# A hybrid diffusion layer on one core: new order of the FFN's head and turn, 19 of its 20 full pairs by Strassen's scheme, activations reloaded on GpSimd's queue

## The reference, cut to what matters

```
def _convffn(h, rows, l, p):
    up = jnp.einsum('bld,df->blf', h, p['ffn_w_up'][l])      # 1024 -> 2 x 2816
    up = _dwconv3(up, p['ffn_conv_w'][l], rows)              # width-3 conv along tokens
    gate, val = jnp.split(up, 2, axis=-1)
    return jnp.einsum('blf,fd->bld', jax.nn.silu(gate) * val, p['ffn_w_down'][l])
...
    x = x + g2 * _convffn(h, rows, l, p)
...
    y_sample = _rmsnorm(xs, final_norm_w)
```

## Time and profile before

| what | value |
|---|---|
| median of 3 runs | 944.24 us (943.34 to 944.41) |
| the profiled execution: time | 944.79 us |
| its span, first to last instruction | 943.0 us |
| PE busy | 901.4 us (96%) |
| DVE busy | 699.2 us (74%) |
| ACT busy | 438.0 us (46%) |
| mean granted TensorE clock | 0.986 |

### The profile page before, as it was taken

One profiled execution on the slowest core, in us unless ns is written; L12 is line 12 of the kernel. 1 busy time (PEld: TensorE's weight loads), 2 busy tenths in 40 slices (PEclk: granted clock), 3 DMA queues, 4 the chain that ended last, 5 costly groups with the idle time before them and its releaser, 6 DMA issues. The chain is left out here.

```text
span 943.0 us, 14067 instructions
## 1 busy us (share of the span) xinstructions
PE 901.4 (96%) x5410; PEld 797.9 (85%) x5410; DVE 699.2 (74%) x884; ACT 438.0 (46%) x713; POOL 39.1 (4%) x58
## 2 busy tenths in 40 slices
PE   7999999999999999999996999999999999987997
PEld 3479898898998988687795999999999999975885
DVE  5744666957858856898678798789779878976536
ACT  5754433333433333232656555555555555553353
POOL 2100000100000000001000000000000000000000
PEclk9999999999999999999997999999999999998999
DMA  9664323423422353218021213322331332215813
GB/s 321 210 219 150 127 75 135 132 79 126 146 95 90 135 179 89 107 24 223 0 90 53 101 59 126 117 87 91 104 118 64 136 110 98 73 65 190 278 48 113
DMA packets 39275, 112.76 MB, mean 120 GB/s; under 512 B 4471, under 2 KB 12663, under 8 KB 38568
## 3 DMA queue, kind: packets, MB, share of 16 engines
q1 hardware_dynamic: 33944, 93.58, 29.1%
q0 software_dynamic: 4800, 17.99, 6.2%
q10 hardware_dynamic: 464, 0.30, 0.1%
HBM read 101.48 MB, written 10.37 MB: 119 GB/s over the span
## 5 line engine op out<-in xcount | busy, mean ns | idle before, releaser
L1981 PE MATMUL ps<-h_hi,w_hi 128*128 128x320 f32 x704 | 223.0, 317 | 11.5 <-issue 9.4
L1983 PE MATMUL ps<-h_hi,w_lo 128*128 128x320 f32 x704 | 218.1, 310 | 0.0
L1982 PE MATMUL ps<-h_lo,w_hi 128*128 128x320 f32 x704 | 218.1, 310 | 0.0
L1981 PEld LDWEIGHTS ps<-h_hi,w_hi 128*128 128x128 f32 x704 | 133.1, 189 | 12.9 <-issue 11.9
L1982 PEld LDWEIGHTS ps<-h_lo,w_hi 128*128 128x128 f32 x704 | 133.0, 189 | 0.2
L1983 PEld LDWEIGHTS ps<-h_hi,w_lo 128*128 128x128 f32 x704 | 132.7, 189 | 0.0
L1852 DVE TENSOR_TENSOR w_lo<-raw,w_hi 128x1024 fp32r<-128x1024 f32 (+1 forms) x56 | 66.3, 1187 | 37.6 <-ACT w_hi L1208 36.4
L1208 ACT ACTIVATE w_hi<-raw 128x1024 fp32r<-128x1024 f32 (+1 forms) x56 | 57.0, 1021 | 52.4 <-PE ps L1983 34.9
L1361 DVE TENSOR_TENSOR w_lo<-raw,w_hi 128x1024 fp32r<-128x1024 f32 x44 | 53.5, 1225 | 6.5 <-ACT w_hi L892 5.4
L1182 ACT ACTIVATE cf<-xf,vec 128x640 f32<-128x640 f32 x44 | 36.4, 828 | 43.7 <-DVE xf L1879 26.8
L1832 DVE SCALAR_TENSOR_TENSOR cf<-xf,vec,cf 128x630 f32<-128x630 f32 x44 | 38.5, 874 | 21.3 <-ACT cf L1184 20.6
(11 more groups left out here) (318 smaller groups left out, 2002.7 us busy)
## 6 DMA issues: line engine op xcount, KB each, us to landing
raw<-in_slots SPq DMA_DIRECT2D x138, 512.0 KB, 4.7
acts<-actf POOLq DMA_DIRECT2D x22, 320.0 KB, 2.4
xf<-acts SPq DMA_DIRECT2D x22, 320.0 KB, 3.7
raw<-in_slots SPq DMA_DIRECT2D x24, 256.0 KB, 5.9
xin<-in_x_sample SPq DMA_DIRECT2D x4, 512.0 KB, 11.0
grow<-gates POOLq DMA_DIRECT2D x2, 1024.0 KB, 12.4
x<-in_x_sample POOLq DMA_DIRECT2D x2, 1024.0 KB, 13.8
out_y_sample<-x SPq DMA_DIRECT2D x4, 512.0 KB, 3.1
```

Source lines behind the costliest of these rows:

```text
L1981: mm(out, lhs[0], rhs[0], start=first, stop=False)
L1982: mm(out, lhs[0], rhs[1], start=False, stop=False)
L1983: return mm(out, lhs[1], rhs[0], start=False, stop=last)
```

## The change

1. `PLAIN` goes from (0, 1, 2, 7, 12, 17) to (0, 1, 2): pairs 7, 12 and 17 become fast, 19 fast pairs in place of 16.
2. The head on ACT and DVE is written out anew: the splits of pair 2's weights (slots 1, 3, 2), the middle and outer taps, the token blocks and the sums of pair 3's weights are interleaved, and the first steps of pair 2 are no longer a `pair_step`. `fast_pair` waits for three token blocks before P6 and for the fourth only before P4.
3. The turn: the last down block of the first pass (the one for `down_step(20)` and `(21)`) goes into slot 1 instead of slot 3, right behind `round_act(20)`. Pass B's blocks use the slots in the order 0, 3, 2, 1 (`B_SLOTS`). Two double blocks (0 and 1), for three token tiles each, stand between the two down steps on PE. The reload, rounding and splitting of activations 0 to 4 move ahead of the taps of pair 21, and DVE takes up only two tiles of the first pass's output at first and three later.
4. The reloads leave SP's queue for POOL's, with seven buffers (three in `wsum`, four in `xf`) instead of four; SP only fetches weights. The first seven reloads stand behind the spill of activation 20 and before that of 21.

The core of the diff, in the order constants, slots, SP, POOL, DVE in the head, DVE in the turn, PE:

```
-PLAIN = (0, 1, 2, 7, 12, 17)
+PLAIN = (0, 1, 2)
...
-    return out + [(NF - 1, 2), ("B", 0), ("B", 1), (NF, 3)] + [("B", m) for m in range(2, PAIRS_DOWN)]
+    return out + [(NF - 1, 2), (NF, 1)] + [("B", m) for m in range(PAIRS_DOWN)]
+B_SLOTS = (0, 3, 2, 1)
...
+                name, value = (("prod_made", product_count(NF - 1, P2)), ("down_step", NF - HEAD_PAIRS),
+                               ("prod_made", product_count(NF - 1, P3)), ("down_made", NT))[slot] if slot < 4 else ("b_done", slot - 3)
...
+        AGAIN = 7
+        def again(f):
+            f %= AGAIN
+            return ap(wsum, f * T, [(1, T)]) if f < 3 else xf[:, (f - 3) // 2, (f - 3) % 2, :]
...
-            first_b = PLACE["down", 1, 0]
-            fetch(5, first_b)
-            for m in range(PAIRS_DOWN):
-                fetch(first_b + m, first_b + m + 1)
-                for f in (2 * m, 2 * m + 1):
-                    eng.wait_ge(sem(f"spilled{f % 2}"), 16 * (f // 2 + 1))
-                    if f < 4:
-                        eng.wait_ge(sem("fconv"), 2 * (NF - 1 + f // 2))
-                    else:
-                        eng.wait_ge(sem("b_split"), f - 3)
-                    load(xf[:, f % 4 // 2, f % 2, :], acts[f], f"ld_a{f % 4}")
+            fetch(5, len(STREAM))
...
+            def reload(f):
+                eng.wait_ge(sem(f"spilled{f % 2}"), 16 * (f // 2 + 1))
+                if f < 3:
+                    eng.wait_ge(sem("lo_ready"), SPLIT[NF - 1, 2])
+                elif f < AGAIN:
+                    eng.wait_ge(sem("fconv"), 2 * (NF - 1 if f < 5 else NF))
+                else:
+                    eng.wait_ge(sem("b_split"), f - AGAIN + 1)
+                load(again(f), acts[f], f"ld_a{f % AGAIN}")
             for t in range(NF):
+                if t == NF - 1:
+                    for f in range(AGAIN):
+                        reload(f)
                 eng.wait_ge(sem("act_ready"), t + 1)
                 load(acts[t], actf[:, t % 2, :], f"spilled{t % 2}")
+            for f in range(AGAIN, NF):
+                reload(f)
+                if f == AGAIN + 1:
+                    load(fnw[:, :], io["final_norm_w"].partition_broadcast(P), "ld_fnw")
...
+            for q in range(3):
+                make_t(q)
+            ffn_lo(HEAD_PAIRS, 1)
             outer_pair(0, 1)
-            make_t(2)
+            make_t(3)
             outer_pair(0, 0)
             split_t(0)
-            make_t(3)
             gated(0)
+            ffn_lo(HEAD_PAIRS, 3)
+            ffn_lo(HEAD_PAIRS, 2)
+            split_act(0)
             split_t(1)
-            split_act(0)
             split_t(2)
             outer_pair(1, 1)
+            outer_pair(1, 0)
+            weight_sums(HEAD_PAIRS + 1, 0)
+            weight_sums(HEAD_PAIRS + 1, 1)
+            gated(1)
+            ffn_lo(HEAD_PAIRS + 1, 1)
+            ffn_lo(HEAD_PAIRS + 1, 0)
+            split_act(1)
+            weight_sums(HEAD_PAIRS + 1, 2)
             split_t(3)
-            ffn_lo(HEAD_PAIRS, 1)
-            if HEAD_PAIRS not in PLAIN:
-                ffn_lo(HEAD_PAIRS, 0)
-            ffn_lo(HEAD_PAIRS, 3)
-            for t in range(HEAD_PAIRS, NF):
+            outer_pair(HEAD_PAIRS, 1)
+            ffn_lo(HEAD_PAIRS + 1, 3)
+            for t in range(HEAD_PAIRS + 1, NF):
                 pair_step(t)
...
-            outer_pair(NF - 1, 0)
-            split_again(0)
-            split_again(1)
-            gated(NF - 1)
-            ffn_lo("B", 2)
-            split_act(NF - 1)
+            ffn_lo("B", 1)
             split_again(2)
             split_again(3)
+            outer_pair(NF - 1, 0)
+            ffn_lo("B", 2)
+            gated(NF - 1)
+            split_act(NF - 1)
+            split_again(4)
...
             down_step(NF - 2)
             down_again(0, range(3))
+            down_again(1, range(3))
             down_step(NF - 1)
             down_again(0, range(3, NT)).then_inc(sem("b_done"), 1)
+            down_again(1, range(3, NT)).then_inc(sem("b_done"), 1)
-            for m in range(1, PAIRS_DOWN - RESIDENT):
+            for m in range(2, PAIRS_DOWN - RESIDENT):
```

More of the change, by code:

```diff
@@ L298, in raw_last @@
     if a == 0:
-        return SPLIT[min(2 * b + 3, NF), 3]
+        return SPLIT[2 * b + 3, 3] if 2 * b + 3 < NF else SPLIT[NF, 1]
     return SPLIT["B", b]
@@ L593, in split_source @@
                 return arrived(eng, ("down", 1, slot))
+            if t == NF:
+                return arrived(eng, ("down", 0, PAIRS_DOWN - 1))
             if slot == 3:
                 down = arrived(eng, ("down", 0, (t - HEAD_PAIRS) // 2))
-                if t == NF:
-                    return down
                 if t in PLAIN:
@@ L1238, in pair_step @@
                     ffn_hi(t + 1, 1)
+                else:
+                    ffn_hi(NF, 1)
                 if plain:
@@ L1250, in pair_step @@
                     middle_tap(t, 1)
-                ffn_hi(t + 1, 3)
+                if t + 1 < NF:
+                    ffn_hi(t + 1, 3)
                 if plain:
@@ L1285, in _ @@
             modulate_tile(4)
-            take_head(2)
-            take_head(3)
-            take_head(4)
+            for j in range(2, 5):
+                take_head(j)
+            first_banks = [bank for bank, _ in UP_BANKS[HEAD_PAIRS]]
+            ffn_hi(HEAD_PAIRS, 1)
             middle_tap(0, 1)
@@ L1883, in pair_step @@
                 fast, next_fast = t not in PLAIN, t + 1 < NF and t + 1 not in PLAIN
-                if t > HEAD_PAIRS and t - 1 not in PLAIN:
+                if t - 1 not in PLAIN:
                     product_sum(t - 1, C12)
@@ L1932, in _ @@
-            if HEAD_PAIRS not in PLAIN:
-                ffn_lo(HEAD_PAIRS, 0)
-            ffn_lo(HEAD_PAIRS, 3)
-            for t in range(HEAD_PAIRS, NF):
-                pair_step(t)
-            if NF - 1 not in PLAIN:
-                product_sum(NF - 1, C12)
-            outer_pair(NF - 1, 0)
-            split_again(0)
-            split_again(1)
-            gated(NF - 1)
-            ffn_lo("B", 2)
-            split_act(NF - 1)
+            outer_pair(1, 0)
+            weight_sums(HEAD_PAIRS + 1, 0)
@@ L1948, in _ @@
+            ffn_lo("B", 2)
+            gated(NF - 1)
+            split_act(NF - 1)
+            split_again(4)
             eng.wait_ge(sem("ld_gate2"), 16)
-            for i in range(NT):
+            for i in range(2):
                 eng.wait_ge(sem("down_made"), i + 1)
                 add(i, 0, "down_taken", "down_added")
+            for f in range(5, 8):
+                split_again(f)
             ffn_lo("B", 3)
-            for f in range(4, 8):
-                split_again(f)
+            for i in range(2, NT):
+                eng.wait_ge(sem("down_made"), i + 1)
+                add(i, 0, "down_taken", "down_added")
@@ L2486, in down_step @@
             def down_step(t):
-                slot_ready(t + HEAD_PAIRS if t + HEAD_PAIRS < NF else NF, 3)
+                slot = 3 if t + HEAD_PAIRS < NF else 1
+                slot_ready(min(t + HEAD_PAIRS, NF), slot)
                 eng.wait_ge(sem("a_ready"), t + 1)
```

97 lines of the change are left out of this document (47 added, 50 removed).

## The result

The changed kernel takes 930.24 us (median of 4 runs, 928.05 to 931.56) where the kernel before takes 943.79 beside it (943.31 to 944.41). The ratio is 0.9854, interval 0.9832 to 0.9875: 13.5 us faster. Forecast was 926.5, with 924 to 929 as the forecast's own range and 922.5 to 932.5 as the stated one: the result lies in the second and not in the first. The profiled execution takes 930.9 us with a span of 929.1, where the forecast for one was 927.1 and 925.3.

What follows compares the result with a forecast made beforehand. PE, busy 96%, ends every chain, but DVE was taken to pace rows of fast pairs; +3.7 pairs, -8.2 head and -13.2 turn sum to -17.7, giving 927.1 for the profiled execution, median 926.5, own range 924 to 929, stated 922.5 to 932.5.

Steps and rivals of the forecast that it cites:

- Term 1, the pairs: Pairs, activation 2 to 20: DVE sets 16.58 us a step, so three new fast pairs cost 3.7 us net.
- slower loop: Rival for the pairs: each of 18 steps takes 17.0 us, costing 7.5 us more, time 934; chance 0.08.
- slower than before: Rival for the pairs: DVE waits each step for a late PE and PE for DVE; 949 at 17.8 a step; chance 0.03.
- DVE keeps up: Rival for the pairs: PE is the bound at 15.75 us a pair, time 910; chance 0.03.
- The upper bound of 17.0: Pairs: slowest step allowed, in us, with half a microsecond of slack used up each time, against 16.58 taken.
- Term 2, the head: Head's end: DVE's new order starts the gating of activation 2 8.2 us earlier; only that is passed on.
- Term 3, the turn: Turn between the passes: with reloads gone from SP, PE's stalls and half clock vanish, 13.4 us less, taken as 13.2.
- the 1.3 us of slack: Turn: low part of activation 21 ready at 851.5, PE comes at 852.8; the tightest place of the change.
- the rival of late reloads: Turn: first reloads land 5 us later than 3.7 after issue, PE stands 3.7 us, time 932; chance 0.11.
- One of the signs: Turn: the prediction is wrong if ACT waits for a reload beyond 836 in the new times.

Runs made afterwards that it cites:

- The shortened sums: Changed kernel with two half-width sums of weights on DVE made over 32 columns instead of 512 from pair 4 on (output not the layer's): 914.95 us, ratio 0.9674.
- the doubled sum: Changed kernel with the third sum of weights on DVE made twice in each later fast pair, result unchanged: 943.3 us, ratio 0.9975.
- SP held back: Changed kernel with SP waiting again before pass B's weight blocks 1 and 2, reloads still on POOL: 936.09 us, ratio 0.9899.
- the three mixtures tried: Changed kernel with 19 fast pairs, 929.29 us; with 7, 12, 17 plain (16 fast), 925.61 us; with 6, 10, 14, 18 plain (15 fast), 926.97 us.

## Why the prediction was right, and what it missed

**Term 1, the pairs, +3.7: right, and shown.** The claim was that DVE's chain, not PE, sets 16.58 a step. The shortened sums give steps shorter by just what they save until PE binds at 15.74; the doubled sum gives steps longer by 0.74; plain pairs give 1.32 each back. It is linear on both sides, so the rivals "slower loop" and "slower than before" (lockstep) fall, as does "DVE keeps up" (it would need DVE to lose 0.83 us a pair). The upper bound of 17.0 was too cautious.

**Term 2, the head, -8.2: right.** The gating of activation 2 is 8.2 us earlier counted from the head's start, PE has no gap, and before P5 of pair 3 it waits 1.54 us (matmuls start at 531.24 and 532.93, 0.147 would be usual), where 1.5 was said. Restoring the old order costs 9.4 to 10.1.

**Term 3, the turn, -13.2: right to 0.3.** Both down steps follow at full clock. The step of it that was too good is the landing of the first reloads: 3.7 us was the median over all reloads of pass B, which moved 133 GB/s; here one of the first lands 4.95 us after its issue, in a stretch at 218 GB/s, and the medians are 4.9 and 5.9. ACT waits 2.84 us for the first, and that uses up the 1.3 us of slack before `down_step(21)`: PE stands 0.4 us. That is the rival of late reloads in small; it needed landings 5 us late to come true, and they were 1 to 2 late. One of the signs that the prediction named for being wrong did come: ACT waits for reloads beyond 836 in the forecast's times. The first wait ends at 838.27, which is 834.7 there, but three more end between 851.9 and 858.4 and last up to 3.31 us. PE doesn't stand for them; the sign was too strict.

**What the sum left out.** 446.53 against 446.3 forecast for the segment (463.96 - 17.7), but 930.9 against 927.1 for the execution: 3.5 of the missing 3.8 us lie ahead of the head, nearly all of them in the mixer's output projection, in code that is the same. How much of it arises where is told by an operation of DVE ahead of that stretch, before and after:

```profile
426.82 0.29 DVE L1715 TENSOR_SCALAR h_hi<-x,vec 128x128 fp32r<-128x128 f32 x1
```

```profile
427.20 0.29 DVE L1732 TENSOR_SCALAR h_hi<-x,vec 128x128 fp32r<-128x128 f32 x1
```

From it to the start of the head (472.06 and 475.59) it is 45.24 us before and 48.39 after. So 3.15 of the 3.53 us arise here, and 0.38 earlier. All profiled executions with the mixer as it was fall into three groups:

| half clock in the output projection | executions | from `h_hi<-x,vec` to the head, us |
|---|---|---|
| 3.4 us, from 434 to 438 on | the kernel before and five others | 45.2 to 45.3 |
| 3.4 us, from 443 on | one (SP held back) | 46.7 |
| 6.8 us, from 443 to 445 on | six | 48.4 |

The changed kernel stands in the first group in one execution and in the third in the other, so it isn't the kernel that decides. The other part is set in the first 40 us of an execution and changes little from there on (0.35 us at most): that operation of DVE comes 0.4 to 2.2 us later than in the kernel before in every other profiled execution, 1.85 in the changed kernel's second one. With these 1.85 taken off, its span of 927.4 is 925.5, where 925.3 was forecast. The forecast was counted from one execution of before that had both the earliest start of all fourteen and the half clock where it costs least. What makes the first 40 us differ stays open.

The stretches of after:

```profile
427.00:443.50 16.50, 13.02 (x75) 11.11 (x75) 15.06 (x27) 5.57 (x14) 0.81 (x2) 1.00 1.10 282
443.50:450.30 6.80, 6.80 (x23) 5.74 (x22) 2.09 (x4) 0.30 (x1) 0.00 (x0) 0.50 0.05 19
```

and of before, the same time and where it had its own:

```profile
434.50:437.90 3.40, 3.40 (x12) 2.94 (x12) 3.23 (x7) 1.35 (x4) 0.00 (x0) 0.50 1.11 246
443.50:450.30 6.80, 6.80 (x36) 5.79 (x35) 2.88 (x4) 1.64 (x4) 0.00 (x0) 1.00 0.03 8
```

23 matmuls against 36 in the same 6.8 us. In before the half clock fell into a stretch in which PE waits anyway, after it fell into one where PE is the bound. The page of before showed such a stretch at 434.5; that it may move from one execution to the next was not in the profile, and there is no term for it in the sum or in the forecast's own range of 924 to 929, which the result misses by 1.2 us. The stated range held it because it had been stretched for another cause, the late reloads. That is luck; the three terms are not.

## What to carry to other kernels

An engine that is busy 99.7% need not be the bound: look at the interval between equal events of the engine that feeds it. Where its work per round is longer, cutting the "busy" engine's work (Strassen) makes things worse, and a mixture in which both need the same is best: from 16.58 - 1.32 p for DVE and 15.74 + 1.76 p for PE the estimate is p = 0.27 plain pairs. Of the three mixtures tried, the one with a plain pair in four has the shortest segment; more plain pairs were not tried. Compare such kernels by a segment that starts behind what differs from execution to execution, or by many executions. And a queue that stands at a wait holds back everything behind it: order what it carries by when it is needed, before thinking of a second queue.

## What the runs showed of the hardware that I had not expected

- Two elementwise operations with both inputs in SBUF, one on GpSimd and one on DVE, ran as if one after the other, not side by side: taps of 0.87 us took up to 2.77. GpSimd's own sums took 1.75 us for 128x512 beside DVE's work, where DVE takes 0.69.
- Reloads of 320 KB landed in 3.7 us as a median on SP's queue before and in 4.9 and 5.9 on GpSimd's; in the kernel with the reloads on SP again, in the stretch of the turn (825 to 865), reloads and weights have medians of 8.2 to 8.5, and nothing is lost by it, as they are issued early enough.
- The granted clock fell to half already during an idle stretch of PE and stayed there behind it, for different times: 10.2 us in all at an idle of 9.42 us in the kernel before, 13.7 at the same idle in the one with the old head, 6.8 at an idle of 5.35. In the mixer of after, an idle of 1.45 us (up to 443.09), the last of several, was followed by 6.8 us. The short stop of the turn (0.24 us idle) was followed by none.
- The same kernel had its half clock in the mixer for 3.4 us in one execution and for 6.8 in another, some 7 us later. The second costs 3.1 us more, since PE is the bound there.
